# Weights as the stationary operand in the feed-forward layers of four row tiles

## The reference

```python
D_FF_2 = int(math.ceil(8 * D_MODEL / 3 / 128)) * 128          # 2816

def swiglu(y, wg, wu, wd):
    return (jax.nn.silu(y @ wg) * (y @ wu)) @ wd

def ffn_sublayer(s, mod, j, g_pre, g_post, wg, wu, wd):
    y = adaln_in(s, g_pre, mod[..., 3 * j, :, :], mod[..., 3 * j + 1, :, :])
    return adaln_out(s, swiglu(y, wg, wu, wd), g_post, mod[..., 3 * j + 2, :, :], FFN_RES)
```

## Time and profile before

| | us |
|---|---|
| median of 3 executions | 2564.03 (2563.63 to 2567.45) |
| profiled execution, whole | 2570.65 |
| its span, first to last instruction | 2568.8 |
| PE busy in it | 2464.2 (96%) |
| VectorE, ScalarE, GpSimd busy | 1145.1, 1064.4, 167.4 |

### The profile page before, as it was taken

How to read it: one execution, slowest core, us unless ns; L and a number is a source line. 1 busy time by engine, 2 the same in 40 slices (tenths; PEclk the granted TensorE clock), 3 DMA queues, 4 the chain that set the end, 5 groups by cost and what they waited for, 6 DMA issues and landing times. The chain is left out here.

```text
span 2568.8 us, 29909 instructions
## 1 busy us (share of the span) xinstructions
PE 2464.2 (96%) x11536; PEld 1939.5 (76%) x11536; DVE 1145.1 (45%) x1960; ACT 1064.4 (41%) x1945; POOL 167.4 (7%) x205
## 2 busy tenths in 40 slices
PE   8999999999999999999989999999999999987998
PEld 6766777766877778877677777887778887766777
DVE  5554455634552223354745222345222335455455
ACT  6443456434542223344545222334222334454544
POOL 1100003000010000022101000001000001310000
PEclk9999999999999999999989999999999999997999
DMA  5557654387534533232103444332432222312554
GB/s 207 184 205 286 229 180 141 123 302 281 189 125 163 173 122 99 91 114 66 58 25 131 157 171 163 100 107 74 174 109 95 99 87 94 115 58 74 172 181 147
DMA packets 118733, 364.40 MB, mean 142 GB/s; under 512 B 11072, under 2 KB 11712, under 8 KB 118592
## 3 DMA queue, kind: packets, MB, share of 16 engines
q1 hardware_dynamic: 116336, 355.62, 40.4%
q0 software_dynamic: 2256, 6.86, 1.1%
HBM read 361.35 MB, written 1.09 MB: 141 GB/s over the span
## 5 line engine op out<-in xcount | busy, mean ns | idle before, releaser
L1478 DVE TENSOR_TENSOR wlo<-raw,whi 128x1024 fp32r<-128x1024 f32 x524 | 644.0, 1234 | 620.1 <-ACT whi L1003 615.5
L562 PE MATMUL ps<-whi,xhi 128*128 128x512 f32 x2096 | 854.6, 408 | 12.5 <-DVE xlo L1570 5.0
L562 PE MATMUL ps<-whi,xlo 128*128 128x512 f32 x2096 | 823.6, 393 | 0.0
L562 PE MATMUL ps<-wlo,xhi 128*128 128x512 f32 x2096 | 821.8, 392 | 0.0
L1003 ACT CAST whi<-raw 128x1024 fp32r<-128x1024 f32 x524 | 549.2, 1051 | 511.0 <-PE ps L562 502.5
L562 PEld LDWEIGHTS ps<-whi,xhi 128*128 128x128 f32 x2096 | 397.9, 190 | 151.8 <-issue 66.1
L562 PEld LDWEIGHTS ps<-whi,xlo 128*128 128x128 f32 x2096 | 396.4, 189 | 87.9
L562 PEld LDWEIGHTS ps<-wlo,xhi 128*128 128x128 f32 x2096 | 398.2, 190 | 73.4
L562 PE MATMUL ps<-whi,ahi 128*128 128x512 f32 x952 | 375.8, 395 | 12.0 <-DVE alo L1701 7.7
L562 PE MATMUL ps<-whi,alo 128*128 128x512 f32 x952 | 373.1, 392 | 0.0
L562 PE MATMUL ps<-wlo,ahi 128*128 128x512 f32 x952 | 372.9, 392 | 0.0
(11 more groups left out here) (153 smaller groups left out, 1409.4 us busy)
## 6 DMA issues: line engine op xcount, KB each, us to landing
raw<-in_w SPq DMA_DIRECT2D x524, 512.0 KB, 3.8
mraw<-in_w_mod SPq DMA_DIRECT2D x72, 1024.0 KB, 6.6
grow<-gains POOLq DMA_DIRECT2D x11, 512.0 KB, 5.3
x<-in_x SPq DMA_DIRECT2D x2, 512.0 KB, 5.2
x<-in_ctx SPq DMA_DIRECT2D x1, 1024.0 KB, 7.8
out<-x SPq DMA_DIRECT2D x2, 512.0 KB, 2.6
rmask<-in_rmask SPq DMA_DIRECT2D x1, 768.0 KB, 4.9
ws<-in_ws POOLq DMA_DIRECT2D x2, 256.0 KB, 5.9
```

What stands on the lines that cost most here:

```text
L562: return nc.tensor.matmul(o, lhsT, rhs, start=start, stop=stop, skip_group_check=True)
L1478: nc.vector.tensor_tensor(wlo[:, slot, :], raw[:, slot, :], whi[:, slot, :].bitcast(F32), ALU.subtract).then_inc(w_split, 1)
```

## The change

In the three sub-layers with `tw` 4, chunk 0 stays as it was. Chunks 1 to 10 (`across(s, c)`) are done in one pass over all 512 rows, `across_pass`: the stationary operand is now a 128 x 128 piece of the weights, and all 512 rows of `xhi` or `xlo` move. The result has the hidden units in the partitions at once. A chunk gives two pairs of banks; a pair holds the gates of 128 hidden units in one bank and the ups in the other, and the pairs go round through the banks (0, 1), (6, 7), (4, 5).

- PE no longer makes the transposes of chunks 1 to 10. It makes the same number of 128 x 512 matmuls, in another order: for each slice `k` six for the first pair and six for the second.
- ScalarE takes silu of a whole bank into `pgate` (`pair_gate`), VectorE multiplies it by the other bank and writes `hid` directly (`pair_out`). The copy out of PSUM (`hidden_out`) goes for these chunks.
- The first bank pair is handed over six matmuls ahead of the chunk's end (`pair_done`), the second with the chunk's last matmul (`unit_done`). PE waits for `pair_taken` before it writes to a pair again, and before the tall stage.
- In ScalarE's and VectorE's order the work on the pairs stands between the splitting of the third and of the fourth unit of the next chunk.
- The modulation steps follow their unit, which is now gone through once, so they are spread evenly and not only over the TRAIL passes.

```diff
+def across(s, c=1):
+
+    return s["kind"] == "ffn" and s["tw"] == 4 and c > 0
+
+
+def pair_banks(q):
+
+    return ((0, 1), (6, 7), (4, 5))[q % 3]
...
+            def across_pass(s, c):
+
+                for u in range(4):
+                    unit = s["u_wide"] + 4 * c + u
+                    slot = unit % RING
+                    pe.wait_ge(w_split, unit + 1)
+                    for kk in range(2):
+                        k = 2 * u + kk
+                        for pair in range(2):
+                            q = 2 * (c - 1) + pair
+                            if k == 0 and q >= 3:
+                                pe.wait_ge(pair_taken, s["pair0"] + q - 2)
+                            elif k == 0 and q < 2:
+
+                                pe.wait_ge(chunk_taken, LEAD4 + TAKEN[s["i"], 0, LEAD])
+                            elif k == 0:
+                                pe.wait_ge(chunk_taken, LEAD4 + TAKEN[s["i"], 0, TRAIL])
+                            for part, b in enumerate(pair_banks(q)):
+                                c0 = CH * kk + 256 * part + P * pair
+                                hi, lo = (w[:, slot, c0:c0 + P] for w in (whi, wlo))
+                                mm(bank(b), hi, xhi[:, k, :], k == 0, False)
+                                mm(bank(b), hi, xlo[:, k, :], False, False)
+                                last = mm(bank(b), lo, xhi[:, k, :], False, k == KD - 1)
+                            if k == KD - 1 and pair == 0:
+                                last.then_inc(pair_done, 1)
+                    last.then_inc(unit_done, 1)
+                    modulation(unit)
+                    if u == 1 and c == 1:
+                        gate_transposes(s, 0, TRAIL)
...
                 if g == 0:
                     pe.wait_ge(chunk_taken, LEAD4 + TAKEN[s["i"], s["chunks"] - 1, st])
+                    if across(s):
+                        pe.wait_ge(pair_taken, s["pair0"] + 2 * s["chunks"] - 3 + st)
...
+            def pair_gate(s, c, pair):
+                q = 2 * (c - 1) + pair
+                if pair == 0:
+                    act.wait_ge(pair_done, s["pair0"] // 2 + c)
+                else:
+                    act.wait_ge(unit_done, DONE[s["u_wide"] + 4 * c + 3, TRAIL])
+                if q < 2:
+                    act.wait_ge(gate_done, LEAD4 + s["silu0"] + s["tw"])
+                else:
+                    act.wait_ge(pair_taken, s["pair0"] + q - 1)
+                nc.scalar.activation(pgate[:, pair, :], bank(pair_banks(q)[0]), ACT.Silu).then_inc(pair_silu, 1)
...
+            def pair_out(s, c, pair):
+
+                q = 2 * (c - 1) + pair
+                dve.wait_ge(pair_silu, s["pair0"] + q + 1)
+                nc.vector.tensor_tensor(hid[:, 2 * c + pair, :], pgate[:, pair, :], bank(pair_banks(q)[1]),
+                                        ALU.mult).then_inc(pair_taken, 1)
...
+                    for u in range(4):
+                        if u == 3:
+                            pair_out(s, c, 0)
+                            pair_out(s, c, 1)
+                        if last:
+                            share_lo(s, s["groups"][0][u], LEAD)
+                            split_lo(s["u_tall"] + u)
+                        else:
+                            split_lo(s["u_wide"] + 4 * c + 4 + u)
```

More of the change, by code:

```diff
@@ L64, in plan @@
         subs.append(dict(kind="ffn", blk=2, l=l, j=2, tw=t, tt=t, chunks=GU_CHUNKS, k=KF))
-    unit = silu = a = xs = f = f_act = 0
+    unit = silu = a = xs = f = f_act = pairs = 0
     for i, s in enumerate(subs):
@@ L85, in plan @@
         s["groups"] = [list(range(sum(sizes[:g]), sum(sizes[:g + 1]))) for g in range(len(sizes))]
-        s["silu0"] = silu
-        silu += s["tw"] * s["chunks"] * (s["kind"] == "ffn")
+        s["silu0"], s["pair0"] = silu, pairs
+        silu += s["tw"] * (1 if across(s) else s["chunks"]) * (s["kind"] == "ffn")
+        pairs += 2 * (s["chunks"] - 1) * across(s)
         s["a0"] = a
@@ L110, in progress @@
         for c in range(s["chunks"]):
+            for u in range(4 if across(s, c) else 0):
+                count += 1
+                done[s["u_wide"] + 4 * c + u, LEAD] = done[s["u_wide"] + 4 * c + u, TRAIL] = count
             for st in (LEAD, TRAIL):
@@ L272, in build @@
         sgate = at("sgate", [P, 4, 256], F32, r_g)
+        pgate = at("pgate", [P, 2, 512], F32, r_g)
         wT = at("wT", [P, 2, 2, 512], F32, r_g)
@@ L352, in build @@
         chunk_taken = sem("chunk_taken")
+        pair_done = sem("pair_done")
+        pair_silu = sem("pair_silu")
+        pair_taken = sem("pair_taken")
         silu_done = sem("silu_done")
@@ L728, in tall_pass @@
                     last.then_inc(unit_done, 1)
-                    if g == 0 and st == LEAD and s["kind"] == "ffn" and k == (0 if len(tiles) == 2 else 1):
+                    if g == 0 and st == LEAD and s["kind"] == "ffn" and not across(s) and k == (0 if len(tiles) == 2 else 1):
                         gate_transposes(s, s["chunks"] - 1, TRAIL)
@@ L1014, in share_hi @@
                 row = s["rows"][k]
+                if across(s) and row >= 2:
+                    act.wait_ge(pair_taken, s["pair0"] + row - 1)
                 nc.scalar.copy(ahi[:, w * aslot:w * aslot + w], src[:, row, P * tiles[0]:P * tiles[0] + w]).then_inc(a_hi_done, 1)
@@ L1164, in hidden_out, with wide_across @@
                     nc.scalar.copy(hid[:, 2 * c:2 * c + 2, P * t:P * t + P], src).then_inc(chunk_taken, 1)
+            def pair_gate(s, c, pair):
[9 more added lines that the diff above has]
+                nc.scalar.activation(pgate[:, pair, :], bank(pair_banks(q)[0]), ACT.Silu).then_inc(pair_silu, 1)
+            def wide_across(s):
+                for c in range(1, s["chunks"]):
+                    if c == 1:
+                        silus(s, 0, TRAIL)
+                        hidden_out(s, 0, TRAIL)
+                    last = c == s["chunks"] - 1
+                    for u in range(4):
+                        if u == 3:
+                            pair_gate(s, c, 0)
+                            pair_gate(s, c, 1)
+                        if last:
+                            share_hi(s, s["groups"][0][u], LEAD)
+                            split_hi(s["u_tall"] + u)
+                        else:
+                            split_hi(s["u_wide"] + 4 * c + 4 + u)
             def proj_out(s, c, st):
@@ L1213, in wide @@
                 ffn = s["kind"] == "ffn"
-                for c in range(s["chunks"]):
+                for c in range(1 if across(s) else s["chunks"]):
                     if c and ffn:
@@ L1243, in wide @@
                             split_hi(s["u_tall"] + k)
-                if ffn:
+                if across(s):
+                    wide_across(s)
+                elif ffn:
                     silus(s, s["chunks"] - 1, TRAIL)
```

18 lines of the change are left out of this document (17 added, 1 removed).

## The result

| | us |
|---|---|
| median of the changed kernel, 4 executions | 2535.19 (2532.03 to 2536.77) |
| median of before, 4 executions | 2565.62 (2563.63 to 2567.45) |
| ratio | 0.988, 95% interval 0.9863 to 0.9897 |
| predicted | 2534.8 (2529 to 2543) |

What follows compares the result with a forecast made beforehand. PE's instruction list was taken to bound the wide stages. Transposes 29.2 us and the old wait 1.0 us go, a new wait adds 1.0: 29.2 us off 2564.03 gives 2534.8 us, range 2529 to 2543 for 8 in 10.

Steps and rivals of the forecast that it cites:

- What bounds the kernel: In the three wide stages PE is busy throughout at clock 1.00, so only shortening or quickening its list saves time.
- Size of a group: Four transposes on PE, two such groups per changed chunk: 0.486 us each by starts, 60 groups, 29.2 us removed.
- The last group: At each sub-layer's last transposes PE also waited for VectorE's `hrow`: 0.35 us each, 1.0 us in all, removed too.
- Step of the matmul: Each chunk's 96 matmuls of 128 x 512 still take 0.2266 us each after the operands change places.
- rival B: Matmul steps lengthen with weights stationary: 10.1 ns more over 2880 uses up the gain, 13.4 ns gives 2573.4 us; 3%.
- New wait at the tall stage: PE's first tall matmul needs banks 0 and 1 0.14 us too early: 0.35 us each, +1.0 us for three.
- Hand-over: First pair's silu and product end 1.73 us after T, the start of that pair's last matmul; no wait inside layers.
- 1.22 us of room: Inside a layer the pair is ready at T + 1.73, needed by the next chunk's seventh matmul at T + 2.95.
- the chain: From the pair's last matmul through ScalarE's silu (0.59 us) to VectorE's product (0.68 us), ending at T + 1.73.
- Modulation: The 40 modulation steps keep their cost, 1.08 us each and 0.11 in the step behind; PE's request stays 1.3 us clear.
- the 4 us of the range: Allowance for the 40 modulation steps costing 0.1 us more or less each: 4 us either way.
- The median: Median of whole executions falls by 29.2 us, from 2564.03 to 2534.8 us, 1.1% less.

Runs made afterwards that it cites:

- the first comparison: The changed kernel against the kernel before: 2535.19 us against 2565.62, ratio 0.988.
- the second: The unaltered changed kernel measured again, on one chip with three of its variants, against the kernel before: 2531.52 us against 2563.79, ratio 0.9875.

## Why the prediction was right

- **What bounds the kernel.** Right. The windows of before showed PE without a gap, and removal from its list came back one for one.
- **Size of a group.** 0.486 us predicted from six groups in 68.18 us; the plain chunk fell by 0.97 us, 0.485 a group, and four transposes put back brought exactly the old chunk. The step from durations (1.1 us) to starts was the one on which the number hung.
- **The last group.** The sum had 0.486 + 0.35 us for it, and that is right for the change, where transposes and wait both go. The kernel with the transposes left out shows that the two overlap: at that place the transposes alone give nothing.
- **Step of the matmul.** 0.2266 us with either operand stationary, in 2880 matmuls; this was an assumption without a row, bounded by rival B, and it held to under 1 ns.
- **New wait at the tall stage.** 0.35 us at the place that was read, as predicted, and the trace has idle time of PE in front of the first tall matmul in all three layers. The layers fell by 9.6, 9.7 and 9.6 us, 28.9 in all, against 29.2. The other 0.3 us were not traced further.
- **Hand-over.** T + 1.75 against T + 1.73; silu 0.598 against 0.59, product 0.688 against 0.68. The prediction's 1.22 us of room left out the 0.10 us from VectorE's end to PE's start. The room is real: 0.65 us more cost nothing, 1.36 us more cost about what the chain says.
- **Modulation.** 1.225 us a step, where the kernel before has 1.22 by the same reading (the prediction's 1.08 + 0.11 us were of the two nearest steps alone). PE waits at none of them: the 4 us of the range weren't needed.
- **The median.** Part of its closeness is luck. The medians moved by 30.4 us in the first comparison and by 32.3 in the second, the layers by 28.9; the remaining 1.5 to 3.4 us are scatter of code that is the same in both. The prediction put the scatter of the medians at 1 us or so, but the two medians of the changed kernel, 2535.19 and 2531.52, are 3.7 us apart. The profiled spans moved by 33.8 us, of which 5.0 lie outside the three layers.

What the Trainium skill tells of a kernel that goes round PSUM banks ("TensorE: Matmul & The Clock Gate", "A second HAM failure mode: psum-queue depth-cycling"), short pauses of PE between groups of matmuls and a clock that goes up and down, did not happen here: the clock is 1.00 in all windows of the new pass, and also with 1 us of idle time in each chunk. No run here has more frequent pauses.

## What to carry to other kernels

Where PE has no gaps, the price of an instruction is the difference of starts between a stretch with it and one without, not its duration: a transpose of 128 x 128 recorded at 0.27 us was worth 0.12, and nothing where it stood beside a wait that stayed. Transposing by swapping the operands cost nothing here with 512 columns moving, and with 256 it still came out level (a chunk of 11.52 us for one of 11.66); what it adds are hand-overs, and whether they are free was decided by where they stand in ScalarE's in-order list, which can be reckoned before (chain length against the number of matmuls until the bank is needed again). To judge effects under the scatter of whole executions, read the trace between two landmarks inside the changed layer.

## What the runs showed of the hardware

The scatter between executions goes with the mean granted clock of the core. Of fifteen executions of the kernel before on one chip, the five at a clock of 0.986 took 2558.41 to 2561.02 us, and the one at 0.980 took 2570.78. The same shows across the kernels: the rest of the span, with the same instructions in most of them, ran from 1467.3 us at a clock of 0.987 to 1484.0 us at 0.980:

```profile
core 0: 2524.8 us, clock 0.987
```

```profile
core 0: 2568.8 us, clock 0.980
```

If PE bounds the stretches at the lower clock, 0.007 less of mean clock is 0.007 of the span: 18 us of 2568.8, an estimate from these two rows. The rests differ by 16.6 us. One of the places is the turn into sub-layer 7. Two microseconds of it each, of before and then of the change, where the granted clock is the number before the DMA share:

```profile
1792.00:1794.00 2.00, 2.00 (x9) 1.81 (x8) 1.67 (x4) 1.56 (x5) 0.52 (x1) 0.50 0.49 4
```

```profile
1769.00:1771.00 2.00, 2.00 (x11) 1.86 (x10) 1.40 (x4) 1.30 (x4) 0.63 (x1) 0.76 0.49 4
```

In both kernels PE had idled before it, for some 4 us, waiting for `rows`. In the kernel before, the first matmuls of the layer still ran at the 1.2 GHz level (starts at 1792.82, 1793.40 and 1793.82); in the change the clock was back when the first one started, at 1770.02. The code there is the same. The fifteen executions show that the clock differs from one execution to the next of one kernel. That the kernel has no part in it is not shown: the ten executions with four transposes put back are all at 0.985 or 0.986, the eight of the changed kernel at 0.982 to 0.984.
